# Second block rounds as seven block products, with bias rows on four partitions

## What is computed

```python
def expert_block(args):
    xe, e = args
    gu = xe @ w_gate_up[e] + b_gate_up[e]
    gate = jnp.minimum(gu[:, :D_FF], SWIGLU_LIMIT)
    up = jnp.clip(gu[:, D_FF:], -SWIGLU_LIMIT, SWIGLU_LIMIT)
    act = (up + 1.0) * gate * jax.nn.sigmoid(SWIGLU_ALPHA * gate)
    return act @ w_down[e] + b_down[e]
```

```python
xc = centred_dwconv(xr, conv_w[l], conv_b[l])
rnn = (rg_lru(xc, wa[0], ba[0], wx[0], bx[0], lam[0], False)
       + rg_lru(xc, wa[1], ba[1], wx[1], bx[1], lam[1], True))
rnn = rnn * jax.nn.gelu(gr)
gates = jax.nn.sigmoid(g_merge)
mix = g_attn * attn + g_rnn * rnn
h = h + mix @ w_out[l]
# rg_lru: r, i = two sigmoid gates from 128x128 block products of xc
#   a = exp(RG_C * r * log_sigmoid(lam));  u = sqrt(1 - a*a) * (i * xc)
#   h[t] = a[t] * h[t-1] + u[t]
```

## Time and profile before

| | us |
|---|---|
| median of 3 runs | 3601.25 (3592.3 to 3604.31) |
| profiled execution, its own time | 3594.6 |
| its span in the trace | 3592.7 |
| expert stage, first to last matmul of the loop | 1240.2 to 2433 |
| attention of the second block, end | 2830.4 |
| eight rounds, first to last matmul | 2832.2 to 3090.8 |
| output product | 3093.7 to 3153.9 |
| PE busy | 3310.1 (92% of the span) |
| DVE, ACT, Pool busy | 1261.4, 726.1, 293.5 |

### The profile page before, as it was taken

The page is one execution under the profiler, slowest core; times in us unless marked ns, Lnnn a source line. Parts: engine busy times, 40 slices in busy tenths (PEclk is TensorE's granted clock), DMA queues, the critical chain, the costliest instruction groups (busy, mean ns, idle before and its releaser), DMA issues.

```text
span 3592.7 us, 41318 instructions
## 1 busy us (share of the span) xinstructions
PE 3310.1 (92%) x14166; PEld 1950.0 (54%) x14167; DVE 1261.4 (35%) x2008; ACT 726.1 (20%) x1242; POOL 293.5 (8%) x231
## 2 busy tenths in 40 slices
PE   7989999999999699999999999995888999999999
PEld 3545555565687433333333333332766788878887
DVE  1354544554445411111111111114556445343342
ACT  2212121221121111111111111111222254211100
POOL 0121221331000000000000000001000011000000
PEclk8999999999999799999999999996899999999999
DMA  4030221333513499999999998893100111312211
GB/s 188 1 123 27 95 65 58 97 123 128 188 47 119 158 345 385 393 379 393 388 394 377 388 381 294 301 347 128 54 0 0 53 68 65 150 47 82 82 71 50
DMA packets 189924, 631.71 MB, mean 176 GB/s; under 512 B 19072, under 2 KB 56064, under 8 KB 179104
## 3 DMA queue, kind: packets, MB, share of 16 engines
q1 hardware_dynamic: 166032, 568.91, 42.6%
q0 software_dynamic: 10944, 39.85, 3.2%
q10 hardware_dynamic: 12880, 22.01, 1.7%
HBM read 594.26 MB, written 36.44 MB: 176 GB/s over the span
## 4 chain that ended last, share of the span: by engine, by line
PE 78%; issue 6%; DMA 6%; DVE 6%; POOL 2%; ACT 2%; SPq 1%; DVEq 0%; ACTq 0%; PEld 0%; POOLq 0%; PEldq 0%
PE ps L301 18%; PE ps L2013 16%; PE ps L260 14%; PE ps L1989 10%; PE ps L1708 6%; DMA slot<-in_w_exp 5%; PE ps L1777 3%; PE ps L1787 1%; PE ps L1753 1%; PE ps L2155 1%; PE ps L415 1%; PE ps L1984 1%; PE ps L1658 1%; PE ps L2174 1%; DVE row_max L2723 1%
## 5 line engine op out<-in xcount | busy, mean ns | idle before, releaser
L2013 PE MATMUL ps<-slot,xT_blk 128*64 128x512 f32 x3200 | 746.6, 613 | 61.6 <-DMA slot<-in_w_exp 51.8
L2013 PEld LDWEIGHTS ps<-slot,xT_blk 128*64 128x64 f32 x3200 | 219.8, 140 | 513.6 <-issue 381.2
L2646 DVE TENSOR_TENSOR gate<-ps,b_row 128x512 f32<-128x512 f32 x50 | 34.6, 692 | 1008.3 <-PE ps L2013 1008.3
L1989 PE MATMUL ps<-slot,aT 128*64 128x512 f32 x1632 | 360.2, 594 | 0.9 <-ACT aT L1515 0.9
L260 PE MATMUL ps<-xnT,slot 128*128 128x264 f32 x1408 | 326.6, 393 | 14.6 <-DVE attnT L1011 6.7
L1708 PE MATMUL ps<-hT,slot 128*128 128x512 f32 (+1 forms) x896 | 310.0, 504 | 1.1 <-ACT small L1312 1.1
L260 PEld LDWEIGHTS ps<-xnT,slot 128*128 128x128 f32 x1408 | 273.1, 194 | 64.7 <-issue 9.1
L1989 PEld LDWEIGHTS ps<-slot,aT 128*64 128x64 f32 x1632 | 117.8, 137 | 234.3 <-issue 234.3
L1708 PEld LDWEIGHTS ps<-hT,slot 128*128 128x128 f32 x896 | 169.5, 192 | 131.1 <-issue 122.1
L2280 DVE SCALAR_TENSOR_TENSOR conv<-ps,g_conv,conv 128x510 f32<-128x510 f32 (+1 forms) x224 | 133.4, 631 | 199.1 <-ACT conv L1325 195.7
L301 PE MATMUL ps<-in_t,in_s 128*128 128x264 f32 x528 | 124.8, 386 | 0.5 <-issue 0.5
(11 more groups left out here) (451 smaller groups left out, 4203.4 us busy)
## 6 DMA issues: line engine op xcount, KB each, us to landing
slot<-in_w_exp SPq DMA_DIRECT2D x768, 512.0 KB, 10.3
in_w<-in_w_ffn SPq DMA_DIRECT2D x22, 1024.0 KB, 4.8
expert_rows<-zero SPq DMA_DIRECT2D x4, 4608.0 KB, 22.4
slot<-in_w_xbc SPq DMA_DIRECT2D x8, 2048.0 KB, 10.2
w_modT<-in_w_modT POOLq DMA_DIRECT2D x32, 512.0 KB, 3.9
b_row<-in_b_gu SPq DMA_DIRECT2D x64, 256.0 KB, 13.3
slot<-in_w_rnn SPq DMA_DIRECT2D x16, 1024.0 KB, 4.8
expert_rows<-y_row ACTq DMA_DIRECT2D x102, 128.0 KB, 5.9
```

The costliest lines, as they stand in the source:

```text
L1989: last = pe.matmul(ps[h * UNIT:(h + 1) * UNIT, 6, :], aT[:, t, d * UNIT:(d + 1) * UNIT], slot[4 + d][:, t * D + h * 512:t * D + (h + 1) * ...
L2013: last = pe.matmul(ps[h * UNIT:(h + 1) * UNIT, 2 * s + t, :], xT_blk[:, k, s * UNIT:(s + 1) * UNIT], slot[i // 4][:, at:at + 512], start=( ...
```

## The change

Three edits.

1. The eight rounds use `Fast` in place of `Dense`: 16 pairs of tiles, two pairs a round, seven products a pair. The data sums `t1` to `t4` are made once by Pool, before the rounds, and the weight sums by Pool too, eight a round, with a step counter of their own (`sums`). The joins stand on ACT (copies) and DVE (adds). A third set of banks is not there (`c` is None): p2 of a pair takes the bank that p1 of the pair before had. The rounds are written out (no loop), a round's recurrence is made one round later, and four tensors have two buffers. The weights of the first four pairs and the first gate weights are loaded before attention. `out2` makes the first seven of eight inner steps of four tiles ahead of its wait for the last round. `norm2_2` uses bank 0.
2. The bias rows go to 4 partitions (0, 32, 64, 96) of a small buffer `b_few`, 4 KB each, in four DMAs; for each unit DVE copies them to the 32 partitions of their quarter (`stream_shuffle` to `b_row`), ahead of its wait for `gu15`. Pool clears `b_few` once.
3. Pool clears `gate[1]` behind the first gather of token rows, in place of DVE.

```diff
@@ Fast
+            if c is None:
+                order = ["p1_0", "p2_0", "p5_0"]
+                for i in range(n):
+                    more = i + 1 < n
+                    order += [f"p6_{i}"] + ([f"p1_{i + 1}"] if more else []) + [f"p7_{i}"] + ([f"p5_{i + 1}"] if more else [])
+                    order += [f"p4_{i}", f"p3_{i}"] + ([f"p2_{i + 1}"] if more else [])
...
+            self.sums = Steps(sem(f"{name}_sums"), order_sums) if order_sums else self.dve
...
+        def bank_2(self, i):
+            return self.bank(self.a, i + 1) if self.c is None else self.bank(self.c, i)
...
         def p1(self, pe, i, loaded):
             pe.wait_ge(*loaded)
-            if i >= 2:
+            if self.c is None:
+                if i:
+                    self.dve.after(pe, f"done11_{i - 1}")
+            elif i >= 2:
                 self.last.after(pe, f"done21_{i - 2}")
...
         def p2(self, pe, i):
-            if i:
+            if self.c is None:
+                if i:
+                    self.last.after(pe, f"done21_{i - 1}")
+            elif i:
                 self.dve.after(pe, f"done11_{i - 1}")
@@ load_bias (SP)
-                sp.dma_start(b_row[h * UNIT:(h + 1) * UNIT].rearrange("p t f -> p (t f)"),
-                             io["b_gu"][bass.ds(e * 2 + h, 1), :].partition_broadcast(UNIT)).then_inc(s_brow, 16)
+                for p in range(h * UNIT, (h + 1) * UNIT, 32):
+                    sp.dma_start(b_few[p:p + 1].rearrange("p t f -> p (t f)"), io["b_gu"][bass.ds(e * 2 + h, 1), :]).then_inc(s_brow, 16)
...
-            sp.wait_ge(moe_dve.sem, moe_dve.before("up", u))
+            sp.wait_ge(moe_dve.sem, moe_dve.before("spread", u))
@@ expert stage (DVE)
         moe_dve.open(dve)
-        dve.wait_ge(s_hrows, 16 * TT)
-        dve.memset(gate[1][:], 0.0).then_inc(s_gate_zero, 1)
...
-                dve.wait_ge(s_brow, e * 32 + 32)
+                dve.wait_ge(s_brow, e * 64 + 64)
+                dve.wait_ge(moe_dve.sem, moe_dve.before("up", u))
+                dve.memset(b_there[:], 0.0)
+                moe_dve.done(dve.stream_shuffle(b_row[:], b_few[:], [0] * 32), "spread")
+                dve.wait_ge(moe_dve.sem, moe_dve.at("spread", u))
@@ rounds (SP)
-        rnn_in.load(sp, load_rg)
-
-
+        for i in range(4):
+            load_rnn(i)
+        sp.dma_start(w_rg[:], row(io["w_rg"], 0)).then_inc(s_rg, 16)
         q_in.pe.all(sp)
         out2.load(sp)
+        for i in range(4, RNN_PAIRS):
+            rnn.pe.after(sp, f"p4_{i - 4}")
+            rnn.sums.after(sp, f"s4_{i - 4}")
+            load_rnn(i)
...
@@ rounds (PE)
-        rnn_in.multiply(pe, rg_gates)
-
-        rnn_in.ev.all(pe)
-        out2.multiply(pe, ready=lambda k: rg_dve.after(pe, "out", k))
+        rnn.p1(pe, 0, rnn_ready(0))
+        rnn.p2(pe, 0)
+        rnn.p5(pe, 0)
+        for i in range(RNN_PAIRS):
+            r, odd = divmod(i, 2)
+            more = i + 1 < RNN_PAIRS
+            rnn.p6(pe, i)
+            if more:
+                rnn.p1(pe, i + 1, rnn_ready(i + 1))
+            rnn.p7(pe, i)
+            if odd:
+                rg_gates(r, 0)
+            if more:
+                rnn.p5(pe, i + 1)
+            rnn.p4(pe, i)
+            if odd:
+                rg_gates(r, 1)
+            rnn.p3(pe, i)
+            if more:
+                rnn.p2(pe, i + 1)
...
+        for j in (2, 3):
+            out2_part(j, range(KD - 1))
+        rnn.act.after(pe, f"done21_{RNN_PAIRS - 1}")
+        rnn.dve.after(pe, f"done12_{RNN_PAIRS - 1}")
+        for j in (0, 1):
+            out2_part(j, range(KD - 1))
+        rnn.dve.after(pe, f"out_{LAST}")
+        for j in range(4):
+            out2.pe.done(out2_part(j, [KD - 1]), f"tile{j}")
...
@@ Pool
+        w_o.pe.all(pool)
+        pool.memset(b_few[:], 0.0).then_inc(s_few, 1)
...
         gather(token_u[:, 0:1])
+        pool.memset(gate[1][:], 0.0).then_inc(s_gate_zero, 1)
...
+        q_in.pe.all(pool)
+        kv_in.pe.all(pool)
+        rnn.sum_x(pool, xn_half)
...
+        sums(0)
         attn_dve.all(pool)
...
+        for r in range(RNN_BLOCKS):
+            rnn.sum_12(pool, 2 * r + 1, [rnn_ready(2 * r + 1)])
+            if r:
+                square(r - 1, 0)
+            rnn.sum_3(pool, 2 * r + 1)
+            if r:
+                square(r - 1, 1)
+            rnn.sum_4(pool, 2 * r + 1)
+            if r < LAST:
+                sums(2 * r + 2)
```

More of the change, by code:

```diff
@@ L276, in program, with __init__ @@
     class Fast:
-        def __init__(self, name, n, kh, width, weight, x, t_sum, s_sum, a, b, c, order_dve, order_act=None, early=False):
+        def __init__(self, name, n, kh, width, weight, x, t_sum, s_sum, a, b, c, order_dve, order_act=None, early=False, order_sums=None, beside=None):
             self.n, self.kh, self.width = n, kh, width
@@ L350, in p3 @@
         def p3(self, pe, i):
-            self.dve.after(pe, f"s4_{i}")
+            self.sums.after(pe, f"s4_{i}")
             self.dve.after(pe, f"done22_{i}")
@@ L868, in program @@
     moe_act = Steps(sem("moe_act"), ["aT", "y", "sigmoid"], 1, ahead=2)
-    moe_dve = Steps(sem("moe_dve"), ["gate", "up", "gate_min", "up_clip", "times", "act"], 1, ahead=2)
+    moe_dve = Steps(sem("moe_dve"), ["spread", "gate", "up", "gate_min", "up_clip", "times", "act"], 1, ahead=2)
     moe_xT_pe = Steps(sem("moe_xT_pe"), ["half0", "half1"], 1)
@@ L875, in program @@
     s_brow = sem("s_brow")
+    s_few = sem("s_few")
     s_yrow = sem("s_yrow")
@@ L1224, in _ @@
             load_piece(i, 0)
+        sp.wait_ge(s_few, 1)
         load_bias(0)
@@ new lines, in rnn_first, with x_half, first_11 @@
+        def rnn_first(name, step, i, dst):
+            rnn.pe.after(act, f"{step}_{i}")
+            rnn.act.done(act.activation(dst, rnn.bank(rnn.a, i), ACT.Copy), f"{name}_{i}")
+        def x_half(r, l):
+            c0 = CONV_W // 2 + l * H2
+            return x_pad[r % 2][:, c0:c0 + H2]
+        def first_11(i):
+            r, odd = divmod(i, 2)
+            if r >= 2:
+                rnn.dve.after(act, f"out_{r - 2}" if odd else f"conv{CONV_W - 1}_{r - 2}")
+            rnn_first("first11", "p1", i, merge_attn[r % 2][:, 0:H2] if odd else x_half(r, 0))
@@ new lines, in gates @@
+        def gates(r, d):
+            rg_pe.after(act, f"gates{d}", r)
+            if r:
+                rnn.dve.after(act, f"input{d}_{r - 1}")
+            rnn.act.done(act.activation(halves(r_gate[d][:]), ps[:, 4:6, 0:H2], ACT.Sigmoid, bias=rnn_prm[:, r, 6 + d:7 + d]), f"r{d}_{r}")
+            if r:
+                rnn.dve.after(act, f"scan{d}_{r - 1}")
+            rnn.act.done(act.activation(halves(i_gate[d][:]), ps[:, 6:8, 0:H2], ACT.Sigmoid, bias=rnn_prm[:, r, 8 + d:9 + d]), f"i{d}_{r}")
@@ L1613, in _ @@
+        for d in range(2):
+            exp_tanh(LAST, d)
+        roots(LAST)
         norm2_2.on_act(act)
@@ new lines, in out2_part @@
+        def out2_part(j, ks):
+            for k in ks:
+                for p in range(2):
+                    last = pe.matmul(ps[:, 2 * (j % 4) + p, 0:H2], slot[j // 4][:, (k * 4 + j % 4) * P:(k * 4 + j % 4 + 1) * P],
+                                     attnT[:, k, p * H2:(p + 1) * H2], start=(k == 0), stop=(k == KD - 1))
+            return last
+        pe.wait_ge(out2.loaded[0], out2.first[0] + 16)
+        rnn.dve.after(pe, f"out_{LAST - 1}")
+        rnn.act.after(pe, f"i1_{LAST}")
+        for j in (2, 3):
+            out2_part(j, range(KD - 1))
@@ new lines, in _ @@
+        rnn.act.after(pe, f"done21_{RNN_PAIRS - 1}")
[5 more added lines that the diff above has]
+            out2.pe.done(out2_part(j, [KD - 1]), f"tile{j}")
+        pe.wait_ge(out2.loaded[1], out2.first[1] + 16)
+        for j in range(4, KD):
+            out2.ev.after(pe, f"tile{j - 4}")
+            out2.pe.done(out2_part(j, range(KD)), f"tile{j}")
@@ L2182, in _ @@
+        out2.ev.after(pe, "tile4")
         norm2_2.on_pe(pe)
@@ new lines, in rnn_add, with step, x_half, done_11 @@
+        def rnn_add(name, firstly, step, bank, i, t):
+            rnn.pe.after(dve, f"{step}_{i}")
+            rnn.act.after(dve, f"{firstly}_{i}")
+            rnn.dve.done(dve.tensor_tensor(t, t, bank, ALU.add), f"{name}_{i}")
+        def step(name, r, instruction):
+            rnn.dve.done(instruction, f"{name}_{r}")
+            rnn.dve.after(dve, f"{name}_{r}")
+        def x_half(r, l):
+            c0 = CONV_W // 2 + l * H2
+            return x_pad[r % 2][:, c0:c0 + H2]
+        def done_11(i):
+            r, odd = divmod(i, 2)
+            rnn_add("done11", "first11", "p2", rnn.bank_2(i), i, merge_attn[r % 2][:, 0:H2] if odd else x_half(r, 0))
```

329 lines of the change are left out of this document (203 added, 126 removed).

## The result

| | us |
|---|---|
| before, median of its runs beside these | 3600.78 (3592.3 to 3604.31, 4 runs) |
| after, median | 3563.24 (3559.18 to 3565.69, 4 runs) |
| ratio | 0.9898, 95% interval 0.9878 to 0.9918 |
| after, profiled execution, its own time and span | 3565.69 and 3563.5 |

The kernel is 37.5 us faster. The forecast was 57.7 us less, 3543 us; the measured time lies in the range of 3505 to 3580. One number hides a lot here: the largest term of the sum, the bias rows, brought almost nothing, and the rounds brought more than their term.

What follows compares the result with a forecast made beforehand. PE, busy 92% of the span, was taken as the bound, with waits for expert weights. Terms -32 - 2.7 - 3.5 - 15.7 - 5.8 + 2 = -57.7 took 3594.6 to 3536.9, plus 6.65 for the median: 3543 us; range 3505 to 3580 (0.85).

Steps and rivals of the forecast that it cites:

- if unit times stay (the bias was no cause): Expert stage: sign that the prediction is wrong; stalling units of 26.9 us were to take some 24.8.
- rival D: Expert stage: bias copies lay in SP's idle time, the burst of loads sets the stall; no 32, 3575 us; chance 0.08.
- Bias rows: Expert stage: without the copies the first awaited piece comes 2.1 us earlier in 15 stalling units, 32 us less.
- 1387.97 + 9 x 1.28 + 2.24 = 1401.7 with a free queue: Stalling unit: batch issue, nine pieces at DMA pace and fixed latency give the awaited piece's arrival, against 1403.85.
- 3.2 us of queue an expert: Expert stage: bias copies hold the DMA queue 1.3 us for their bytes and 1.9 more at half rate.
- Rival C: Expert stage: the stalls vanish and the clock stays, -81 in place of -32, 3494 us; chance 0.09.
- Gate half: Start of the expert stage: with the clear on Pool, PE starts when DVE opens its counter, 2.7 us less.
- Entry and attention: Ahead of the rounds: early weights cut wait and half clock, 3.5 us less; Pool's sums slow attention, 2 us more.
- Rounds: Eight rounds: fewer products save 28.5 us, lateness from Pool and DVE excluding each other gives back 12.8; net -15.7.
- The term for p1: Rounds: p1 of the pair after next waits for done11, held by Pool's sums, 1.2 us late once a round.
- Tail: Merge and out2: the merge's wait and the half clock behind it go, 5.8 us less.
- F: Rounds: steps held by Pool delay every join behind them on in-order DVE, kernel slower, 3655 us; chance 0.04.

Runs made afterwards that it cites:

- bias_only: The kernel before with the bias edit alone (four small bias DMAs and a shuffle per unit): 3590.83 us against 3592.45, ratio 0.9987.
- small_sums: The changed kernel with Pool's weight sums, from the second pair on, over 128 of their 512 columns: 3555.09 us, ratio 0.989 to before.
- order_after: The changed kernel, SP loading the next expert's gate/up pieces 0 to 7 ahead of down pieces where an expert has one unit: 3480.34 us, ratio 0.9678.

## Why the prediction held in its range and failed in its largest step

**By its own sign the prediction was wrong.** It said that it is wrong "if unit times stay (the bias was no cause)". They stayed: the 15 stalling units have a mean of 27.29 us, and had 27.58. The time is in the range because the range was made wide enough for a largest term of nothing (rival D, 3575), and because the rounds cost 5 us less than forecast. Of the 57.7 us that were forecast, the part that came is the rounds with what stands around them. That the number lies as near as it does is luck, and says nothing for the largest term.

**Bias rows: wrong.** Forecast -32, measured -4.2 in the traces, which is within their scatter, and -1.6 in bias_only alone. The step that failed is "1387.97 + 9 x 1.28 + 2.24 = 1401.7 with a free queue". That the batch is issued at a fixed place in the unit held (3.57 us behind the turn of gated rows, before and after). That the DMA engines are then ready for it at full rate did not. In after, the batch is issued at 1391.35 and PE gets its piece at 1407.34, 15.99 us later; by the same formula it would be 13.76, and before it was 15.88. The freed queue ran empty, had its first bytes 1.0 us behind the issue (a part of the 2.24), and then moved 333, 250 and 322 GB/s for 5.6 us, until it was back at 414. An estimate from these rates: 1.55 of the 2.23 us too much are that slow rate; the rest is open. What the copies had cost was paid by the empty engines. Rival D had this outcome, but with another reason: not that the bias lay in idle time (its copies did fill the engines, which were full for the whole cycle), but that removing it uncovers a second limit. D put 8 in 100 on it. The profile of before had hints of both: a DMA share of 1.03 over three whole units, with the cycle at 71.1 us, speaks for bytes, and SP's batch, which starts only when PE has used the first down piece, speaks for the order. The prediction read the first at one place and took the second as a number. (Its 3.2 us of queue an expert are 2.7 by the stretch of the earlier trace rows alone, 1.28 and 3.0 x (411 - 212) / 411 = 1.45; the sum doesn't use them.)

Rival C, the end of the stalls (-81), is what happens when both limits go: 79 us in the traces, 83 by the medians, 84 together with the bias edit on the kernel before.

**Gate half: right in size at its place** (0.20 us from the table to PE, -2.7), but the next unit took 1.3 us more at lower clock, which may or may not be its doing, and what remains is beneath what a timing shows.

**Entry and attention.** PE's wait at the entry is 0.96 us, as forecast ("some 1 us"), and the first 32 records take 7.23 us where the full pace is 7.12: the half clock is gone. From the first norm to the start of the rounds it is 0.4 us shorter, forecast -1.8 + 2 = +0.2. DVE's small steps went from a mean of 0.26 to 0.31 us over 48, 2.5 us, and PE's wait for `q_now` from 8.5 to 9.2. Ahead of that, between the last unit and the first norm, 1.9 us more are no part of the forecast: 1.3 are the same products at lower clock (the turn of gated rows 1.12 us for 0.66, `down` of the last unit 9.25 for 8.44), and 0.6 a longer wait for DVE's `moe_tok` (9.65 for 9.07).

**Rounds: the mechanism right, the size smaller.** The product count was exact: 28.48 a round. Of the lateness, 1.6 us a round was forecast and 0.97 measured. The term for p1 was mis-sized: 1.2 forecast, 0.55 measured in seven rounds of eight. conv0 was taken at 0.77 us and takes 0.55 alone, and Pool's sums made conv0 0.54 and conv1 0.88 us longer, not each 1.1. The others had 0.4, and take 0.34, but not from Pool, as small_sums shows; what delays them is open. The rest is 0.08 a round behind the wait at p1, and 0.74 once, in the last round, where PE waits for ACT's `merge_attn`. That the wait at p1 is Pool's doing, it shows too. (The Trainium skill, "GPSIMD Engine Reference", "1. Specifications", has the two engines collide at the SBUF interfaces they share where VectorE reads two SBUF inputs; 1314 ns against 766 agree.) From the start of the rounds to that of `out2` -25.9 us were measured; the forecast for it was -15.7, with -1.7 of half clock and -2.9 of the merge's wait that it counted at entry and tail: -20.3. 5 us of it are the smaller lateness; that comes to -25.3.

**Tail: right.** `out2` takes 57.04 us up to the next product, forecast 57.0. With the 2.9 us of the merge's wait 5.9 us are gone, forecast 5.8.

**Against F**, slower than before: no join is late by more than 0.57 us. What speaks for it, a Pool step that holds DVE's queue, is real; over the rounds DVE is busy 165.77 us in place of 134.99 with small sums, and PE loses 4.5 us.

**The sum.** The traces differ by 29.2 us, 28.5 less than forecast. The bias term makes 27.8 of that. The first 1237 us (+4.5, no part of the change), the first unit (+1.3) and what is behind the last (+1.9) take 7.7 more, the rounds with tail and attention give 6.3 back, and the rest 0.7. That the medians differ by 37.5 us, and so are nearer to the forecast, comes from which executions were profiled and timed: that of before was 6.2 us under its median, that of after 2.4 over. Against the 48 later executions of before it would be 29 us, half of the forecast.

## What to carry to other kernels

Before costing the removal of traffic from a full queue, read two things over a whole cycle of the loop: whether the DMA engines are full all the way and PE still waits (bytes; full alone is no proof, as order_after shows), and what the queue's next issue waits for (order). If both stand at the same height, one edit shows nothing, which doesn't mean that it is worthless: here 2 us and 18 us alone made 84 together. In an in-order queue, put the load whose buffer is free first and is needed first ahead of the one that waits. And an add that a product waits for stands on its engine as early as its inputs allow, which is worth more if another engine can hold the steps ahead of it.
